# Sparse experts of the last layer: results weighted and summed by token in four PSUM banks, three experts' weights resident

## The reference

```python
def grouped_moe(h, router_w, router_b, w_gate, w_up, w_down):
    scores = jax.nn.sigmoid((h @ router_w).astype(jnp.float32))
    biased = scores + router_b.astype(jnp.float32)
    grouped = biased.reshape(biased.shape[:-1] + (N_GROUPS, EXPERTS_PER_GROUP))
    group_score = lax.top_k(grouped, TOP_K)[0].sum(-1)
    best = jnp.argmax(group_score, axis=-1)
    in_group = (best[..., None] == jnp.arange(N_GROUPS))[..., None]
    masked = jnp.where(in_group, grouped, -jnp.inf).reshape(biased.shape)
    _, idx = lax.top_k(masked, TOP_K)
    w = jnp.take_along_axis(scores, idx, axis=-1)
    w = w / jnp.sum(w, axis=-1, keepdims=True)
    combine = jnp.einsum('bnk,bnke->bne', w, jax.nn.one_hot(idx, N_EXPERTS, dtype=jnp.float32)).astype(h.dtype)
    out = jnp.zeros_like(h)
    for e in range(N_EXPERTS):
        he = jax.nn.silu(h @ w_gate[e]) * (h @ w_up[e])
        out = out + combine[..., e:e + 1] * (he @ w_down[e])
    return out
...
        x = x + g2 * grouped_moe(hx2, router_w, router_b, w_exp_gate[l], w_exp_up[l], w_exp_down[l])
...
    return rms_norm(x, final_g)
```

## Time and profile before

| what | value |
|---|---|
| median of three runs | 1762.7 us |
| profiled execution, time | 1764.99 us |
| profiled execution, span | 1763.3 us |
| TensorE busy | 1568.8 us (89%) |
| VectorE busy | 493.0 us (28%) |
| ScalarE busy | 317.8 us (18%) |
| GpSimd busy | 57.2 us (3%) |
| HBM read and written | 359.02 and 16.88 MB |

### The profile page before, as it was taken

The page is one execution under the profiler, slowest core; times in us unless marked ns, Lnnn a source line. Parts: engine busy times, 40 slices in busy tenths (PEclk is TensorE's granted clock), DMA queues, the critical chain, the costliest instruction groups (busy, mean ns, idle before and its releaser), DMA issues.

```text
span 1763.3 us, 20529 instructions
## 1 busy us (share of the span) xinstructions
PE 1568.8 (89%) x8615; PEld 965.3 (55%) x8615; DVE 493.0 (28%) x1143; ACT 317.8 (18%) x713; POOL 57.2 (3%) x69
## 2 busy tenths in 40 slices
PE   5999999999999999599999839999999984977783
PEld 3664645644444448355565518775788873544441
DVE  1222466423342013410111023346334122100002
ACT  2121243211111001100000022434122110100001
POOL 0000000000000000200000010000000001000000
PEclk8999999999999999799999969999999996999997
DMA  9554313133434453679999972321134557999995
GB/s 365 190 198 174 113 36 103 37 114 137 146 105 167 167 210 137 239 290 402 386 384 398 404 279 63 115 74 36 37 108 134 180 225 252 388 387 398 395 399 188
DMA packets 128284, 377.28 MB, mean 214 GB/s; under 512 B 8211, under 2 KB 84941, under 8 KB 113597
## 3 DMA queue, kind: packets, MB, share of 16 engines
q1 hardware_dynamic: 115292, 344.43, 52.5%
q0 software_dynamic: 5216, 16.57, 2.8%
q10 hardware_dynamic: 7680, 14.92, 2.5%
HBM read 359.02 MB, written 16.88 MB: 213 GB/s over the span
## 4 chain that ended last, share of the span: by engine, by line
PE 75%; DMA 17%; DVE 3%; ACT 2%; issue 2%; POOL 0%; ACTq 0%; POOLq 0%; SPq 0%; DVEq 0%
PE ps L1069 14%; PE ps L942 11%; PE ps L1191 11%; PE ps L945 9%; DMA ring<-in_w_exp_up 9%; PE ps L1086 7%; PE ps L881 7%; PE ps L1208 5%; PE ps L894 2%; DMA arena<-moe_rows,idx_all 2%; DMA arena<-in_w_exp_up 2%; PE ps L977 1%; PE ps L972 1%; PE ps L1182 1%; PE ps L995 1%
## 5 line engine op out<-in xcount | busy, mean ns | idle before, releaser
L1069 PE MATMUL ps<-hT,ring 128*128 128x512 f32 (+1 forms) x768 | 262.2, 491 | 1.4 <-ACT arena L1441 1.4
L942 PE MATMUL ps<-hT,ring 128*128 128x512 f32 (+1 forms) x544 | 210.5, 540 | 0.0
L1069 PEld LDWEIGHTS ps<-hT,ring 128*128 128x128 f32 x768 | 142.4, 190 | 115.3 <-issue 105.9
L945 PE MATMUL ps<-ring,hT 128*128 128x256 f32 (+1 forms) x832 | 174.1, 367 | 5.0 <-DVE arena L1696 4.0
L1191 PE MATMUL ps<-ring,arena 128*64 128x256 f32 (+2 forms) x1472 | 151.4, 361 | 19.2 <-DMA ring<-in_w_exp_up 12.3
L1191 PE MATMUL ps<-arena 128*64 128x256 f32 (+2 forms) x1216 | 145.1, 383 | 25.2 <-DMA arena<-in_w_exp_up 14.7
L945 PEld LDWEIGHTS ps<-ring,hT 128*128 128x128 f32 x832 | 147.7, 191 | 33.6 <-issue 16.2
L942 PEld LDWEIGHTS ps<-hT,ring 128*128 128x128 f32 x544 | 101.5, 191 | 98.4 <-issue 93.3
L1191 PEld LDWEIGHTS ps<-ring,arena 128*64 128x64 f32 (+2 forms) x1472 | 92.7, 133 | 78.0 <-issue 38.1
L1086 PE MATMUL ps<-arena,ring 128*128 128x512 f32 (+1 forms) x384 | 133.4, 487 | 0.0
L1191 PEld LDWEIGHTS ps<-arena 128*64 128x64 f32 (+2 forms) x1216 | 87.2, 139 | 81.9 <-issue 40.5
(11 more groups left out here) (216 smaller groups left out, 1271.0 us busy)
## 6 DMA issues: line engine op xcount, KB each, us to landing
ring<-in_w_in SPq DMA_DIRECT2D x54, 1024.0 KB, 6.9
ring<-in_w_ada SPq DMA_DIRECT2D x48, 1024.0 KB, 7.1
ring<-in_w_exp_gate SPq DMA_DIRECT2D x16, 2048.0 KB, 17.1
arena<-in_w_exp_gate SPq DMA_DIRECT2D x16, 2048.0 KB, 22.0
ring<-in_w_exp_up SPq DMA_DIRECT2D x16, 2048.0 KB, 18.5
ring<-in_w_exp_down SPq DMA_DIRECT2D x16, 2048.0 KB, 23.9
arena<-in_w_exp_up SPq DMA_DIRECT2D x16, 2048.0 KB, 22.5
arena<-in_w_exp_down SPq DMA_DIRECT2D x16, 2048.0 KB, 20.9
```

The source lines that it names most:

```text
L942: last = pe.matmul(ps[:, bank, 0:tok.stop - tok.start], w[:, k, at:at + width], hT[:, k, tok], start=(k == 0), stop=(k == KD - 1))
L945: last = pe.matmul(ps[:, bank, 0:width], hT[:, k, P * tok:P * (tok + 1)], w[:, k, at:at + width], start=(k == 0), stop=(k == KD - 1))
L1069: last = pe.matmul(ps[:, 0, lo:TOK], kview(n)[:, k, P * (m % 2):P * (m % 2 + 1)], hT[:, k, lo:TOK], start=(k == 0), stop=(k == KD - 1))
```

## The change

For the last layer alone (`WAYS = (2, 3)`, `CHIP = (0, EXPERTS)`):

- The results of an expert are no longer copied and stored. DVE multiplies them out of PSUM by the g2 row (`g2_half`, halves of the row on the two halves of the partitions) into one of two small buffers.
- DVE builds for each expert two 128 x 128 matrices (`marks`, one for each token tile) that hold the token's weight where the slot is the token's, twice side by side. TensorE turns them (`turn_marks`), ACT keeps them as `marksT`, and TensorE multiplies them with the scaled results (`sum_results`): four products of 64 rows by 512 columns, accumulated over all 16 experts in PSUM banks 4 to 7. The sum of i-2 stands behind gate(i), the turn of marks of i-1 ahead of down(i-1).
- Gate and up share bank 0 (so up(i) waits for silu(i), and gate(i) for the multiplication of i-1), the turned hidden values and marks use bank 3, the down product bank 1, and the turned rows bank 2 alone: `turn_rows` turns 64 instead of 128 rows, and ACT alone keeps them.
- The picks, the wait for the stores, the scaling of picked results and the weights `wsel` are left out; DVE adds the residual straight from two banks for each tile. The weights of all slots (`weight_of`) are computed after the count.
- A third set of weights (`third_set`: the space of `hT` and 16 KB x 2 more of each partition) takes expert 2. SP issues its three tiles ahead of the loop, behind the g2 rows, and each later tile three experts ahead: gate(i+3) at gate(i), up(i+3) at up(i), down(i+2) at down(i-1).
- `fg_row` and `f_tok` move to the space of `ret_tab`; g2 is loaded as half rows.

```diff
+WAYS = (2, 3)
+CHIP = (0, EXPERTS)
+GATE_AT, UP_AT, HID_AT, Y_AT, SUM_AT = ((0, 0), (0, 0)), ((1, 0), (0, 256)), (4, 3), (5, 1), (None, 4)
...
         second_set = [region(20992, 2 * TILE), region(3072, 2 * TILE), region(3072 + 2 * TILE, 2 * TILE)]
+        third_set = [hT_flat, region(11264, 2 * TILE), region(11264 + 2 * TILE, 2 * TILE)]
...
+                if CHIP[l] == EXPERTS:
+                    for half in range(2):
+                        sp.dma_start(g2_half[64 * half:64 * (half + 1), :],
+                                     mod_d[l, 1, 3 * D + 512 * half:3 * D + 512 * (half + 1)].partition_broadcast(64))\
+                          .then_inc(g2_in, 16)
...
+                if WAYS[l] == 3:
+                    sp.wait_ge(logits, before(nq, l + 1))
+                    for j in range(3):
+                        expert_tile(l, 2, j, 2)
...
                 for i in range(EXPERTS):
-                    if i + 2 < EXPERTS:
-                        e = RUN[l][i + 2]
+                    ahead = i + WAYS[l]
+                    if ahead < EXPERTS:
+                        e = RUN[l][ahead]
...
-                    if 1 <= i < EXPERTS - 1:
+                    if i >= 1 and ahead - 1 < EXPERTS:
                         sp.wait_ge(moe.down, EXPERTS * l + i)
-                        expert_tile(l, i + 1, 2, expert)
+                        expert_tile(l, ahead - 1, 2, expert)
...
+                    pe.wait_ge(moe.rowsT_kept, EXPERTS * before(rows_by, l) + rows_by[l] * (i + 1))
+                    if i > 0 and UP_AT[l][0] == GATE_AT[l][0]:
+                        pe.wait_ge(moe.hid, EXPERTS * l + i)
+                    elif EXPERTS * l + i > 0:
                         pe.wait_ge(moe.silu, EXPERTS * l + i)
...
+                    if i > 1 and on_chip(l, i - 2):
+                        sum_results(i - 2)
                     if i > 0:
                         hidden_of_expert(i - 1)
+                    if UP_AT[l][0] == GATE_AT[l][0]:
+                        pe.wait_ge(moe.silu, EXPERTS * l + i + 1)
...
+                def turn_marks(i):
+
+                    pe.wait_ge(moe.marked, l + 1 + nth_on_chip(l, i))
+                    pe.wait_ge(moe.hidT_kept, EXPERTS * l + i + 1)
+                    for t in range(nq[l]):
+                        last = pe.transpose(ps[:, HID_AT[l], 256 + P * t:256 + P * (t + 1)], marks[:, t, :], ident)
+                    last.then_inc(moe.turned, 1)
+
+                def sum_results(i):
+
+                    results_kept(pe, l, i)
+                    pe.wait_ge(moe.turned_kept, nth_on_chip(l, i))
+                    for t in range(nq[l]):
+                        for half in range(2):
+                            r = slice(64 * half, 64 * (half + 1))
+                            last = pe.matmul(ps[:, SUM_AT[l] + 2 * t + half, :], marksT[r, t, :], y_of(l, i)[r, 0:512],
+                                             start=(i == 0), stop=(i == EXPERTS - 1))
+                        if i == EXPERTS - 1:
+                            last.then_inc(moe.summed, 1)
...
-                for j, chosen in ((0, first), (1, second)):
...
+                if CHIP[l] < EXPERTS:
+                    for j, chosen in ((0, first), (1, second)):
+                        step(dve.tensor_tensor(flat(rt_a), flat(score), flat(chosen), ALU.mult))
...
+                def mark_slots(i):
+
+                    if nth_on_chip(l, i) > 1:
+                        dve.wait_ge(moe.turned, nth_on_chip(l, i) - 1)
+                    for t in range(n):
+                        ins = dve.tensor_scalar(marks[:, t, :].rearrange("p (a q) -> p a q", a=2),
+                                                bc(slot_num[:, 0:64].unsqueeze(1), P, 2, 64), slot_of[:, t, i:i + 1],
+                                                weight_of[:, t, i:i + 1], ALU.is_equal, ALU.mult)
+                    ins.then_inc(moe.marked, 1)
...
+                    if on_chip(l, i):
+                        dve.wait_ge(moe.down, k + 1)
+                        dve.tensor_tensor(y_of(l, i), ps[:, Y_AT[l], :], g2_half, ALU.mult).then_inc(moe.y_dve, 1)
...
                     for i in range(n):
-                        combine(i)
+                        dve.wait_ge(moe.summed, i + 1)
+                        total = ps[:, SUM_AT[l] + 2 * i:SUM_AT[l] + 2 * i + 2, :].rearrange("p b c -> p (b c)")
+                        dve.tensor_tensor(res[:, t0 + i, :], res[:, t0 + i, :], total, ALU.add).then_inc(x_done, 1)
```

More of the change, by code:

```diff
@@ L394, in trunk @@
         slot_in = [sem(f"slot{s}_in") for s in range(RING)]
-        expert_in = [[sem(f"expert_{name}{way}_in") for name in ("gate", "up", "down")] for way in range(2)]
+        expert_in = [[sem(f"expert_{name}{way}_in") for name in ("gate", "up", "down")] for way in range(max(WAYS))]
         ada_ready = sem("ada_ready")
@@ L677, in cap_of, with on_chip, nth_on_chip @@
             return CAPS[l][RUN[l][i]]
+        def on_chip(l, i):
+            return EXPERTS - CHIP[l] <= i < EXPERTS
+        def nth_on_chip(l, i):
+            return sum(CHIP[:l]) + i - (EXPERTS - CHIP[l]) + 1
         def stored(l, i):
-            return 16 * (sum(stores(cap_of(m, n)) for m in range(l) for n in range(i % 2, EXPERTS, 2))
-                         + sum(stores(cap_of(l, n)) for n in range(i % 2, i + 1, 2)))
+            return 16 * (sum(stores(cap_of(m, n)) for m in range(l) for n in range(i % 2, EXPERTS, 2) if not on_chip(m, n))
+                         + sum(stores(cap_of(l, n)) for n in range(i % 2, i + 1, 2) if not on_chip(l, n)))
         def all_stored(eng, l):
@@ L686, in all_stored, with y_of, kept_by_dve, kept_by_act @@
                 eng.wait_ge(moe.y[i % 2], stored(l, i))
-        def y_of(i):
-            return y_odd if i % 2 else y_e
-        def in_two_banks(l, i):
-            return sum(c > 64 for m in range(l) for c in CAPS[m]) + sum(cap_of(l, m) > 64 for m in range(i + 1))
+        rows_by = [2 if max(c) > 64 else 1 for c in CAPS]
+        def y_of(l, i):
+            return y_bufs[l][i % 2]
+        def kept_by_dve(l, i):
+            own = lambda m, n: cap_of(m, n) > 64 or on_chip(m, n)
+            return sum(own(m, n) for m in range(l) for n in range(EXPERTS)) + sum(own(l, n) for n in range(i + 1))
+        def kept_by_act(l, i):
+            return sum(not on_chip(m, n) for m in range(l) for n in range(EXPERTS)) \
+                + sum(not on_chip(l, n) for n in range(i + 1))
+        def results_kept(eng, l, i):
+            if not on_chip(l, i):
+                eng.wait_ge(moe.y_act, kept_by_act(l, i))
+            if on_chip(l, i) or cap_of(l, i) > 64:
+                eng.wait_ge(moe.y_dve, kept_by_dve(l, i))
         def expert_weights(l, i, j):
             k = KF if j == 2 else KD
-            return expert_slot(expert_slots[l][j], k) if i % 2 == 0 else second_set[j].rearrange("p (k c) -> p k c", k=k)
+            if i % WAYS[l] == 0:
+                return expert_slot(expert_slots[l][j], k)
+            return (second_set, third_set)[i % WAYS[l] - 1][j].rearrange("p (k c) -> p k c", k=k)
         def weights_in(l, i):
-            return 16 * (EXPERTS // 2 * l + i // 2 + 1)
+            same = lambda m, upto: sum(n % WAYS[m] == i % WAYS[l] for n in range(upto))
+            return 16 * (sum(same(m, EXPERTS) for m in range(l)) + same(l, i + 1))
         def in_slot_before(l, s):
@@ L1167, in _ @@
                     .then_inc(placed, 1)
-                pe.wait_ge(first_marked, l + 1)
+                pe.wait_ge(moe.marked, l + 1 + sum(CHIP[:l]))
                 cap = cap_of(l, 0)
@@ L1197, in turn_hidden @@
                     for c in range(0, cols, P):
[L1198 removed]
+                        last = pe.transpose(ps[:, HID_AT[l], c:c + P], hid_of[l][:, c:c + P], ident)
                     return last
@@ L1539, in _ @@
                         act.wait_ge(moe.hid, k)
-                    act.activation(silu_e[:, 0:cols], ps[:, 0, 0:cols], ACT.Silu).then_inc(moe.silu, 1)
+                    act.activation(silu_of[l][:, 0:cols], ps[:, 0, 0:cols], ACT.Silu).then_inc(moe.silu, 1)
                     if i + 1 < EXPERTS:
@@ L1563, in ready @@
                 tile_done(DEPTH - 1, t - XT)
-            for i in range(nq[DEPTH - 1]):
-                scale_first(DEPTH - 1, i)
             for t in range(XT, NT):
@@ L1974, in _ @@
                 dve.tensor_copy(count_i[:, :], top[:, 0, 0:1]).then_inc(count_ready, 1)
+                if CHIP[l]:
+                    weight_of = flat(biased)
+                    dve.wait_ge(count_ready, l + 1)
+                    step(dve.tensor_tensor(flat(rt_a), flat(score), flat(assign), ALU.mult))
+                    step(dve.tensor_reduce(top[:, 0:n, :], flat(rt_a), AX.X, ALU.add))
+                    step(dve.reciprocal(top[:, 0:n, :], top[:, 0:n, :]))
+                    step(dve.tensor_tensor(weight_of, flat(rt_a), bc(top[:, 0:n, :], P, n, EXPERTS), ALU.mult))
+                    dve.wait_ge(g2_in, 16 * (rows_of[0] + 2))
@@ L2133, in _ @@
```

(5 more changed lines are left out.)

210 lines of the change are left out of this document (128 added, 82 removed).

## The result

The changed kernel took 1736.65 us (median, 1735.48 to 1737.66), the kernel before beside it 1764.56 us (1762.36 to 1766.88): 27.9 us or 1.6% less, ratio 0.9841, 95% interval 0.9824 to 0.9859. The forecast was 1734, its range 1723 to 1748. The profiled execution took 1737.66 us, its span is 1736.0.

The account below looks back on a forecast made before the run. The prediction took weight transfer to bound the last layer's experts. Savings of 9.6 (stores), 0.7 (g2 rows), 5.7 (third set) and 12.8 (tail), 28.8 us, from 1764.99 gave 1736.2, at the median's level 1734; range 1723 to 1748.

Parts of the forecast that it names:

- Bound by transfer: Last layer's experts: weight transfer sets the pace, 16.6 us an expert, while TensorE needs 14.1.
- TensorE's path: From gate(2) at 1511.3 through the last expert at 14.1 us each: down(15) done at 1714.6 if no tile were late.
- The sign named: Late in the stage: 16.6 us from expert to expert, with TensorE waiting for tiles.
- Last tile: Last down tile lands at 1717.0 in place of 1733.0, by 9.6, 0.7 and 5.7 us saved.
- Stores: Fourteen experts' result stores ahead of the last tile go; their transfer time is saved whole, 9.6 us.
- Start: Ahead of the steady stage: third set cuts idle transfer from 13.3 to 7.6 us, 5.7 saved; smaller g2 rows, 0.7.
- The list chain: Scatter and read ahead of expert 1's gather take 8 us longer beside weights; DVE's earlier steps give back 1.45.
- The tail: Behind the last tile: 12.3 us after down(15) in place of 26.6, less 1.5 of added work, 12.8 saved.
- A: Rival: lists starve behind the weights, some 20 us extra in place of 8, giving 1746; chance 0.12.
- B: Rival: TensorE becomes the bound from 14.7 us an expert; at 15.5 the time is 1745; chance 0.12.
- C: Rival: TensorE's clock drops, kernel slower than before; at 0.72 about 1806; chance 0.04.
- D: Rival: the change doesn't take hold; third set only moves idle time, tail's 12.8 lost, giving 1752; chance 0.05.

Follow-up runs that it names:

- lists_first: The changed kernel, with SP waiting for the token lists to be read back before it issues the third set of weights: 1738.51 us, ratio to before 0.9843.
- the tail experiment: The changed kernel, with ACT's root table loaded early and down(15) put ahead of the sum of 14: 1736.64 us, ratio to before 0.9825.
- more_turns: The changed kernel, with the turns of marks done six times over: 1750.63 us, ratio to before 0.9909.
- two_sets: The changed kernel, back on two sets of weights in the last layer, all else kept: 1742.22 us, ratio to before 0.9871.

## Why the prediction came out, point by point

**The sum.** 28.8 us were forecast; between the profiled spans 27.3 came (1763.3 to 1736.0), and the span ends 1.4 us behind the 1734.6 that was named. The median lies 2.7 over the forecast; the other 1.3 is that the profiled execution of before was 2.3 over its median and that of after only 1.0 over its own. The parts follow; one of them, the last tile, is right by luck.

**Bound by transfer: half right.** The stage was bound by transfer before and is now bound by both. The forecast had TensorE's path 7.7 us shorter; it was about 4. The sign named, 16.6 us from expert to expert late in the stage, came as 15.7 for the last three ((1703.54 - 1656.53) / 3). Without its 3.8 us of waits down(15) would have ended at 1720.2, the forecast said 1714.6. Of the 5.6 us, 1.95 is the gather of expert 1, which landed at 1496.45 in place of 1494.5 (1.1 of it because the stage began later), and 13 x 0.22 = 2.9 is the expert at 14.32 in place of 14.1; the other 0.7 I can't place. The term of the expert that was mis-sized is the turns: 64 rows cost 1.02 us, hardly less than 128 rows, 1.09. I had taken 0.85 of bounds 0.55 to 1.09. The sums took 1.92 against 2.0, marks 0.37 against 0.3.

**Last tile: right, by two errors that cancel.** It landed 33.3 us after its issue at 1685.2, at 1718.5; the forecast was 1717.0, and the stage began 1.1 later. The changed kernel's last down tile, issue and time to landing:
```profile
L781 SPq DMA_DIRECT2D ring<-in_w_exp_down x1: 7082/7082/7082, 1685.2 to 1685.2; - x1
...
DMA to landing us min/median/max: 33.3/33.3/33.3
```
Relative to the stage's start it came 15.6 us earlier than before; 16.0 were forecast. But the terms behind it were 9.6 (stores) and 6.4 (start), and the queues show another split. *Stores:* the step that failed is "in a stage bound by transfer both would be saved whole". 3.41 MB fewer stores gave the weights' queue 1.87 MB more in the 210 us from 1506 (75.55 before, 77.42 after), 4.8 us. The experiments priced one copy at 1.1 to 7.5 us, by the measure taken, and two copies at 11 to 12 where twice the term is 19.2: all below the term. The busy share was at 100% in both cases, and I had read that as a fixed budget; it isn't, since the rate under that share went from 386 to 395 GB/s when stores were added (more of this in the last section). *Start:* in 1466 to 1506 the weights' queue moved 12.22 MB in place of 8.62, 9.3 us at 389 GB/s, where I had 5.7 + 0.7. The idle time was longer than the two windows I had read (236 GB/s over 40 us is 15.7 us short of 389, I had counted 13.3), and after it 6.5 us were left in place of 7.6. 9.3 + 4.8 = 14.1, close to the 14.5 us by which the tile came earlier on the span's clock (1733.0 to 1718.5).

**The list chain: right.** 8.7 us longer for the two list steps where I took 8: scatter 11.26 in place of 6.12, read 5.49 in place of 1.93. The price came from the small packets beside 16 KB pieces, not from a row of its own. The part of DVE's steps held (1.47 us earlier, 1.45 forecast). Gate(1) ended at 1504.23, forecast 1502.9. What I hadn't foreseen is that the DMA engines count as fully busy from 1470 to 1478 and yet move 230 GB/s, with 148 GB/s in the second half of that stretch. Weights and list pieces slow each other there: in the four traces in which the last scatter met no third set (before, lists_first and the two with two sets) it took 6.1 to 8.2 us, in the eight in which it met the gate tile of one 10.8 to 12.6. By what mechanism the runs don't show. That moved the dry stretch later and made it shorter (113 GB/s in 1502 to 1506), so in sum it cost no more than forecast.

**The tail: right.** 12.0 us from the end of down(15) to the end of the span, 12.3 forecast. The forecast charged 1.5 for sum(14) and the marks ahead of down(15); the tail experiment took 2.0 off the end, with the order and the table load (1.26) changed together.

**The rivals.** A (20 us of lists) didn't come: 8.7. B (TensorE bound from 14.7 us an expert) came half: the expert was well under 14.7, but the slack was half of what I had, so the point of decision lay at 14.32 + 4/14 = 14.6. more_turns passed it and paid. C (clock): the granted clock was 1.00 in 1506 to 1720, higher than the 0.96 before, with TensorE busy 98% in place of 79%. D didn't come: the third set, with the stores gone, moved the last tile by 15.6 us, and the tail after down(15) fell from 26.6 to 12.0.

## What to carry to other kernels

A busy share of 100% on the DMA engines is not a budget in which each queue's share can be saved in full: price a transfer by what the other queue moves without it (here about half its share for 3.4 MB of stores, two thirds for 6.6 MB). When a change fills the slack of the second resource, cutting either one alone is worth nothing more, and an experiment that relieves both shows what the first would have been worth. List traffic of a few bytes that meets large pieces has its delay, here 8.7 us, and it belongs into the sum. Holding the large pieces back until the lists are through (lists_first) gained nothing here, since the queue stood idle meanwhile.

## What the runs showed of the hardware that I had not expected

- The total rate from 1506 to 1716 rose with a second hardware queue: 386 GB/s with weights and gathers, 395 with 3.41 MB of stores, 399 with 6.64 MB, at a busy share of 1.0 each time. With two sets it was 391 and 402. The kernels with full tiles and no stores lie at 382 to 391, those with stores, the kernel before among them (393), at 393 to 402.
- A gather of 64 rows (0.26 MB) took at most 5.0 us when it was issued 1 us ahead of a 2 MB tile (one trace), and 9.5 and 10.4 us when issued 1.3 and 0.1 us behind one.
- Where small list writes met 16 KB pieces, both sides were slow: the scatter took 11.26 us in place of 6.12, and the weights' queue moved 0.59 MB in the 4 us from 1474, at a busy share of 1.0.
- Turning 64 rows in place of 128 took 1.02 us in place of 1.09: with this shape nearly all of the cost goes by the number of turns (8), not by their width.
- Gate(1) took 5.9 us at a mean granted clock of 0.62 (1498.32 to 1504.22), after 12.4 us in which TensorE was idle but for the turns of rows; the gate product of a later expert took 3.45. The kernel before paid the same, 5.81 us at 0.62, after 7.4 us of idle time. In two_sets, where the gather was early, it took 3.67, so a late gather costs over 2 us more than its delay.
- SP's issue of a tile took 0.33 or 0.38 us from 1504 to 1600 us, though the DMA engines were already busy all the time, and from 1602 on, with tiles three experts ahead, up to 13.97 us. Whatever stands behind a tile on that engine waits too.
